# Sums of squares of two head norms taken as columns, with the squares as the stationary operand

## The reference, cut to what matters

```
y_m = mlstm_mixer(...)    # 4 heads of 64; h = rmsnorm(h, norm_g) over each head's 64 numbers
y_a = diff_attention(...) # 4 heads; rmsnorm of q and k over 64 numbers each, 4*2 heads each
y_h = hgrn2_mixer(...)    # 4 heads of 64; o = rmsnorm(o, norm_g) over each head's 64 numbers
x = x + concat(y_m, y_a, y_h) @ w_out
def rmsnorm(x, g): return x * rsqrt(mean(x*x, -1) + 1e-6) * g
```

## Time and profile before

| | us |
|---|---|
| median of 3 runs | 3740.42 (3738.63 to 3741.89) |
| profiled execution | 3740.01 |
| its span, first to last instruction | 3738.7 |
| mean granted TensorE clock | 0.941 of full |
| PE busy | 3434.8 (92%) |
| DVE, ACT, POOL busy | 1297.9, 1131.7, 1223.0 |

### The profile page before, as it was taken

How to read it: one execution, slowest core, us unless ns; L and a number is a source line. 1 busy time by engine, 2 the same in 40 slices (tenths; PEclk the granted TensorE clock), 3 DMA queues, 4 the chain that set the end, 5 groups by cost and what they waited for, 6 DMA issues and landing times.

```text
span 3738.7 us, 37076 instructions
## 1 busy us (share of the span) xinstructions
PE 3434.8 (92%) x15602; PEld 2733.0 (73%) x15602; DVE 1297.9 (35%) x2104; ACT 1131.7 (30%) x1552; POOL 1223.0 (33%) x305
## 2 busy tenths in 40 slices
PE   7887899998977899999998789998999989769999
PEld 5654588886744688888887678887888867548887
DVE  3336641214256431222124642123221253572122
ACT  2234332322234332322223232223222232423222
POOL 4210044343200244444443334443444432014443
PEclk9887799999977899999999899999999999879999
DMA  3210033332200133333322223323433323013332
GB/s 116 66 52 1 12 101 92 101 92 78 68 30 1 50 98 90 102 95 91 107 83 90 76 72 92 106 82 117 137 91 104 89 74 116 1 40 95 97 97 72
DMA packets 462184, 296.77 MB, mean 79 GB/s; under 512 B 14331, under 2 KB 454193, under 8 KB 462017
## 3 DMA queue, kind: packets, MB, share of 16 engines
q1 hardware_dynamic: 453664, 277.09, 25.5%
q10 hardware_dynamic: 8352, 17.30, 1.3%
HBM read 285.97 MB, written 8.39 MB: 79 GB/s over the span
## 4 chain that ended last, share of the span: by engine, by line
PE 82%; DVE 12%; ACT 3%; POOL 1%; issue 1%; DMA 0%; SPq 0%; ACTq 0%; DVEq 0%; POOLq 0%
PE bank L505 24%; PE bank L506 24%; PE bank L507 24%; PE bank L335 9%; DVE x L794 1%; DVE ta L792 1%; DVE ta L1177 1%; DVE xl L818 1%; POOL wlo L443 0%; DVE qkv L1972 0%; DVE sqacc L812 0%; DVE ta L1969 0%; DVE scr L1722 0%; DVE tiny L1465 0%; DVE u L689 0%
## 5 line engine op out<-in xcount | busy, mean ns | idle before, releaser
L443 POOL TENSOR_TENSOR wlo<-raw,whi 128x2048 fp32r<-128x2048 f32 (+4 forms) x283 | 1187.3, 4196 | 2348.3 <-ACT whi L428 2348.3
L505 PE MATMUL bank<-xh,whi 128*128 128x512 f32 x2432 | 971.4, 399 | 61.7 <-DVE xl L818 38.3
L506 PE MATMUL bank<-xl,whi 128*128 128x512 f32 x2432 | 958.5, 394 | 0.0
L507 PE MATMUL bank<-xh,wlo 128*128 128x512 f32 x2432 | 957.4, 394 | 0.0
L428 ACT ACTIVATE whi<-raw 128x2048 fp32r<-128x2048 f32 (+3 forms) x288 | 503.4, 1748 | 683.4 <-PE bank L507 648.5
L505 PEld LDWEIGHTS bank<-xh,whi 128*128 128x128 f32 x2432 | 463.7, 191 | 178.0 <-DVE xl L818 29.7
L507 PEld LDWEIGHTS bank<-xh,wlo 128*128 128x128 f32 x2432 | 463.0, 190 | 98.7
L506 PEld LDWEIGHTS bank<-xl,whi 128*128 128x128 f32 x2432 | 463.7, 191 | 93.0
L505 PE MATMUL bank<-ah,whi 128*128 128x512 f32 x1216 | 474.6, 390 | 5.2 <-POOL wlo L443 5.2
L506 PE MATMUL bank<-al,whi 128*128 128x512 f32 x1216 | 474.4, 390 | 0.0
L507 PE MATMUL bank<-ah,wlo 128*128 128x512 f32 x1216 | 474.4, 390 | 0.0
(11 more groups left out here) (334 smaller groups left out, 3004.3 us busy)
## 6 DMA issues: line engine op xcount, KB each, us to landing
raw<-in_ffn_w_gate SPq DMA_DIRECT2D x88, 512.0 KB, 4.0
raw<-in_ffn_w_up SPq DMA_DIRECT2D x88, 512.0 KB, 5.3
raw<-in_w_up SPq DMA_DIRECT2D x64, 512.0 KB, 4.8
raw<-in_w_down SPq DMA_DIRECT2D x64, 512.0 KB, 4.9
raw<-in_w_in SPq DMA_DIRECT2D x56, 512.0 KB, 4.7
raw<-in_ffn_w_down SPq DMA_DIRECT2D x64, 384.0 KB, 4.0
raw<-in_ffn_w_down SPq DMA_DIRECT2D x64, 320.0 KB, 3.5
raw<-in_w_out SPq DMA_DIRECT2D x16, 512.0 KB, 4.5
```

The lines of the kernel that those rows point to most:

```text
L443: g.e.tensor_tensor(self.wlo[slot][:, 0:n], self.raw[slot][:, 0:n], self.whi[slot][:, 0:n].bitcast(F32), ALU.subtract).then_inc(self.lo_ma ...
L505: pe.e.matmul(bank, hi[:, at:at + P], xh, start=k == ks[0], stop=False)
L506: pe.e.matmul(bank, hi[:, at:at + P], xl, start=False, stop=False)
L507: last = pe.e.matmul(bank, lo[:, at:at + P], xh, start=False, stop=k == ks[-1])
```

## The change

Where the buffers of squares hold all tiles (mLSTM, HGRN2), TensorE now makes the columns at once: for each block of 128 tokens and each of the two tiles, the squares (128 features by 128 tokens) are the stationary operand and four columns of `C_IND` stream through. That is 8 matmuls of 4 columns in place of 2 of 512 columns and 4 transposes, and the copy L1023 goes. Two turns are taken from each of these norms on each engine. The attention's norm keeps its way. The helper runs for mLSTM and for HGRN2 once in each layer, four times in all.

```diff
@@ act_rstd
         yield
-        yield
-        yield
+        if n < len(tiles):
+            yield
+            yield
         a.wait_ge(v_sig, v_sig[(*tag, "means")])
@@ pe_rstd
         for first in range(0, len(tiles), n):
             yield
             pe.wait_ge(a_sig, a_sig[(*tag, "squares", first)])
+            if n == len(tiles):
+
+                for b in range(NB):
+                    for j in range(n):
+                        last = self.mm(ps[:, b * w:b * w + w], squares[j][:, b * P:b * P + P], self.const[:, C_IND, 16 * j:16 * j + w],
+                                       b == 0 and j == 0, b == NB - 1 and j == n - 1)
+                last.then_inc(pe_sig.tick(*tag, "columns"), 1)
+                continue
...
-        yield
-        pe.wait_ge(v_sig, v_sig[(*tag, "sums")])
-        for b in range(NB):
-            last = pe.e.transpose(ps[:, b * w:b * w + w], rows[0:w, b * P:b * P + P], self.const[0:w, C_IDENT, 0:w])
-        last.then_inc(pe_sig.tick(*tag, "columns"), 1)
+        if n < len(tiles):
+            yield
+            pe.wait_ge(v_sig, v_sig[(*tag, "sums")])
+            for b in range(NB):
+                last = pe.e.transpose(ps[:, b * w:b * w + w], rows[0:w, b * P:b * P + P], self.const[0:w, C_IDENT, 0:w])
+            last.then_inc(pe_sig.tick(*tag, "columns"), 1)
@@ dve_rstd
-        v.wait_ge(pe_sig, pe_sig[(*tag, "sums", first)])
-        v.e.tensor_copy(rows[0:w, :], ps[0:w, :]).then_inc(v_sig.tick(*tag, "sums"), 1)
-        yield
-        yield
+        if n < len(tiles):
+            v.wait_ge(pe_sig, pe_sig[(*tag, "sums", first)])
+            v.e.tensor_copy(rows[0:w, :], ps[0:w, :]).then_inc(v_sig.tick(*tag, "sums"), 1)
+            yield
+            yield
         v.wait_ge(pe_sig, pe_sig[(*tag, "columns")])
```

## The result

| | before | after |
|---|---|---|
| median (12 runs each) | 3739.28 (3736.08 to 3747.87) | 3748.81 (3744.15 to 3752.58) |
| ratio, 95% interval | | 1.0024 [1.0016, 1.0032] |
| profiled execution, its span | 3740.01, 3738.7 | 3748.93, 3747.6 |
| mean granted clock | 0.941 | 0.936 |

The prediction was 3736.0, with a range up to 3744. The time lies outside it, and it moved the other way. It is the number of rival (c), 3748.

A forecast was written before the change was run, and what follows sets the result against it. PE holds 82% of the chain, but the norms are chains of hand-overs with no engine full. A layer: -1.2 - 3.6 + 2.55 = -2.25 us, two layers -4.5, so 3735.5 profiled, 3736 as median; range 3729 to 3744.

The forecast's parts named there:

- rival (c): Lag exposed for both head pairs (5.1 us), near products ahead of the heads' transposes: +8.0 us in all, 3748; chance 0.09.
- The sums themselves: Both norms: new sums cost 1.9 (mLSTM) and 3.4 us (HGRN2), like the old; PE saves only the transposes, 0.4 to 0.6.
- Term 1: mLSTM's norm: earlier sums and reciprocals let the last L1306 start 1.2 us sooner a layer; bounds 0 and 2.
- Term 2: Tail at HGRN2's norm: heads' products no longer wait for squares and sums; L1011 3.6 us sooner a layer, bounds 1.7 and 3.9.
- My test for term 2: Term 2 is wrong if third block's transposes to `out`, 26.1 us, shrinks by less than 2 us.
- Term 3: HGRN2 lags the heads by about one level: hidden beside heads 0 and 1, 2.55 us exposed beside 2 and 3; bounds 0, 5.1.
- The prediction's own sign of being wrong in this term: Maxima of heads 2 and 3 come no later against mLSTM's end than before, or over 4 us later.

The follow-up runs named there:

- e8: Kernel before with columns made at once in mLSTM's and HGRN2's norms, every turn kept, so no other stream's instruction changes place; 3747.34 us, 1.0012 of before.
- g3: Changed kernel with two idle turns ahead of the attention's norm (no lag) and two ahead of HGRN2's norm; 3736.65 us, 0.9984 of before.
- g2: Kernel before with columns for HGRN2's norm alone and two idle turns ahead of that norm, mLSTM's norm as before; 3736.07 us, 0.9984 of before.
- e4: Kernel before with two idle turns ahead of HGRN2 on every engine, so it lags the heads, no columns; 3751.38 us, 1.0022 of before.
- g1: Kernel before with two idle turns ahead of HGRN2's norm, old sums and transposes kept; 3738.77 us, 0.9989 of before.
- g4: g3 with its two idle turns behind the attention's norm instead of ahead, so HGRN2 lags in that norm alone; 3743.12 us, 1.0000 of before.

## Why the prediction was wrong, point by point

**The sums themselves: right, but for what follows them.** 16 records in 1.96 and 1.90 us, within the 1.9 to 3.4 given; mLSTM's in layer 1 took 2.80. HGRN2's I took at 3.4, it was 1.90 in both layers (the second below); in e8, at a clock of 0.50, it was 3.57, so the estimate of 1.7 us at either clock does not hold at the lower one. That the products behind the sums could run at another clock for it, as they do in e8, stood in no term.

**Term 1: right in mechanism and size, worthless in effect.** Counted from the squares, the sum had L1011 at 11.8 us, L1035 at 13.7 and the last L1306 at 22.5; the rows above give 11.66, 13.64 and 22.22, a gain of 1.43 us against 1.2. But in g3, where the two turns stand idle behind it, 0.3 to 0.6 us of it are left at the heads, and g2, without it, is no slower.

**Term 2: right at its head, partly lost at its end.** From the third block's transposes to the heads' products it is 1.18 us, as forecast (1.17); to L1011 it is 432.49 - 421.55 = 10.94 us, where it was 14.29: 3.35 sooner, forecast 3.6. From there to `out` the code is the same, but before it took 11.78 us in layer 0 and 9.10 in layer 1, after it 12.73 in both. Layer 1 before:

```profile
1236.42 1.06 PE L1011 MATMUL bank<-const,scr 128*4 128x128 f32 x4
1238.25 1.12 PE L335 MATMUL bank<-scr,sel 4*128 4x512 f32 x2 [0.77 <-DVE scr L1035]
1239.30 2.05 PE L335 MATMUL bank<-u 128*128 128x128 f32 x16
1241.28 1.12 PE L335 MATMUL bank<-scr,sel 4*128 4x512 f32 x2
1245.52 0.76 PE L505 MATMUL bank<-mh,whi 128*128 128x512 f32 x1 [3.12 <-DVE ml L1306]
```

And after:

```profile
1235.57 1.90 PE L335 MATMUL bank<-const,scr 128*128 128x4 f32 x16
...
1240.87 1.06 PE L1021 MATMUL bank<-const,scr 128*4 128x128 f32 x4
1242.70 2.07 PE L335 MATMUL bank<-scr,sel 4*128 4x512 f32 x2 [0.77 <-DVE scr L1046]
1244.70 3.78 PE L335 MATMUL bank<-u 128*128 128x128 f32 x16
1248.41 2.07 PE L335 MATMUL bank<-scr,sel 4*128 4x512 f32 x2
1253.60 0.76 PE L505 MATMUL bank<-mh,whi 128*128 128x512 f32 x1 [3.12 <-DVE ml L1317]
```

The same three groups took 0.95 + 1.73 + 0.95 = 3.63 us more, each near twice as long: a granted clock of 0.50 where it was 1.00. That is more than the 3.13 us that the tail had gained at its head in this layer. My test for term 2 (26.1 us shrinks by under 2) is passed in layer 0, where it shrinks to 23.67. In layer 1 it fails: 23.70 before (from 1221.82), 24.20 after (from 1229.40). Without the lag the gain of the place does arrive: 0.9984 and 0.9982.

**Term 3: the step that failed.** It had a lag of one level at 2.55 us a layer, all of it beside heads 2 and 3, bounded by 5.1. The runs put the lag at 3748.81/3739.28 against g3's 0.9984, so 0.41%, some 15 us or 7.7 a layer (the intervals leave 5 us either way on the 15); e4 against g1 gives 12 to 15. The prediction's own sign of being wrong in this term, maxima of heads 2 and 3 over 4 us late, is met in layer 0 (5.6 to 9.3) and not in layer 1. The lag has three places:

- The attention's norm, 3.1 us by order and up to 1.6 by the clock. The prediction did not charge it at all. I had moved the heads against HGRN2, but the attention's norm moves with them, and there the lag puts a level in front of the spreading. The diff of the instruction order showed it; I looked for the level only on DVE and among the heads.
- Heads 0 and 1: nothing (3.1 to 3.3 in the table, layer 0). Here the prediction was right, for the reason given: their third maxima are 5.8 us late, and the tables, which now come behind the third block, give 2.5 of it back.
- Heads 2 and 3. The level ahead of the maxima is there as forecast. DVE after, layer 0:

```profile
393.67 0.42 DVE L1720 TENSOR_TENSOR scr<-u,scr 128x256 f32<-128x256 f32 x1
394.00 0.42 DVE L1721 TENSOR_TENSOR scr<-u,scr 128x256 f32<-128x256 f32 x1
394.34 1.32 DVE L1733 COPY_PREDICATED scr<-level,bank 128x512 f32<-128x512 uint8 x2
395.56 0.87 DVE L1476 TENSOR_REDUCE tiny<-bank 128x1 f32<-128x128 f32 x4
...
402.66 1.33 DVE L1733 COPY_PREDICATED scr<-level,bank 128x512 f32<-128x512 uint8 x2 [2.23 <-PE bank L335]
403.89 0.67 DVE L1738 TENSOR_TENSOR scr<-scr,u 128x512 f32<-128x512 f32 x1
...
405.33 0.76 DVE L1476 TENSOR_REDUCE tiny<-bank 128x1 f32<-128x256 f32 x2 [0.17 <-PE bank L335]
...
409.37 0.48 DVE L1488 SCALAR_TENSOR_TENSOR u<-u,tiny 128x256 f32<-128x256 f32 x1
```

It costs 1.2 us at the first maxima and 0.95 more at the second (0.4 in layer 1). What came on top is what I had priced under rival (c) and given 0.09. The weights of the second block are ready at 409.85, and PE then has this ahead of their transposes:

```profile
410.02 2.88 PE L335 MATMUL bank<-scr,u 128*64 128x128 f32 x16 [0.69 <-ACT scr L1819]
412.83 0.80 PE L335 MATMUL bank<-u,scr 128*128 128x128 f32 x2
413.42 0.73 PE L1419 MATMUL bank<-const,u 128*128 128x128 f32 x4
```

Before, the same products had run beside the exponentials, and the transposes started as soon as the weights were there:

```profile
401.53 1.58 PE L335 MATMUL bank<-scr,u 128*64 128x128 f32 x16 [0.69 <-ACT scr L1808]
403.04 0.49 PE L335 MATMUL bank<-u,scr 128*128 128x128 f32 x2
...
404.48 0.48 DVE L1477 SCALAR_TENSOR_TENSOR u<-u,tiny 128x256 f32<-128x256 f32 x1
...
405.02 0.44 PE L1408 MATMUL bank<-const,u 128*128 128x128 f32 x2 [0.36 <-DVE u L1477]
```

That is 413.42 - 409.85 = 3.6 us of exposure, of which 2.8 show at the third maxima. Not all of it is order: 1.30 + 0.31 = 1.6 us are the clock, 0.50 here and 1.00 before. In layer 1 the exposure is 3.5 us, and only 0.3 of it shows, since there the stretch from the weights to the third maxima had run at 0.68 before and took 5.36 us, for 3.92 in layer 0. Against this rival I had argued that the products ran ahead of the scores before. That was read from heads 0 and 1 (322.28); beside heads 2 and 3 they ran behind the scores of the second block, where PE had nothing else to do.

**The sum.** Terms 1 and 2 without the lag measure -6 us (g3), for -9.6; the lag measures +15, for +5.1. -6 + 15 = +9, and the change measures +9.5. (The 15 is the difference of the change and g3, so this shows where the two parts lie and not that they add up; without any columns g1 measured -4 and e4, which is g1 with the lag, +11, each beside its own runs of before.) How much of the 15 is order and how much the clock that came with it stays open: of the places above only the norm's 3.1 us are cleared of the clock. Rival (c) had the right total and one of the right mechanisms (the near products), but 5.1 us for the pairs where 2 were, and not the norm. So it was right by half, and its total by luck.

**The range** went wrong with term 3: its upper bound of 5.1 a layer took the lag as one level's work on DVE, and not as what each queue does at every place where the two lines meet. It did not even take in its own bounds together: no gain from mLSTM, the lesser tail and 5.1 of lag give +3.4 a layer, 3746.8.

## What to carry to other kernels

Where queues are filled by stepping generators in turn, a shorter helper is two changes: the operation, and the shift of everything behind it. Price the shift by going through every engine's order at every later meeting point, the nearest first, and put idle steps back where the operation was to see the two apart. Here the operation gained nothing that could be measured, and at the old place of HGRN2's sums it cost some 2 us a layer by the clock behind it (e8); the shift cost 15 us. The two turns given back and the sums of HGRN2 placed behind the last scores make the version that beats both (3736.65 and 3735.88 us, 0.9984 and 0.9982 of before), and the old sums at that place give most of it.

## What the runs showed of the hardware

The same instructions in the same order take different times in the two layers of one execution, by the clock that each stretch is granted. In g4 the windows of the mixers are

```profile
246.98:442.30 195.32, 135.80 (x697) 83.45 (x697) 119.74 (x274) 86.84 (x172) 0.00 (x0) 0.72 0.01 4
1057.27:1247.99 190.72, 132.99 (x697) 83.36 (x697) 119.53 (x274) 86.77 (x172) 0.00 (x0) 0.74 0.01 4
```

4.6 us apart at 0.72 and 0.74. A single profile of a stretch with many short waits is good to some 5 us, as large as most terms of my sum; the medians and the comparison of both layers are what the conclusions above rest on. Keeping PE busier with matmuls of 64 rows and 64 columns did not raise the clock (0.68 to 0.70). And two ways to make the same sums, of nearly the same length (4 records of 512 columns in 3.35 us, 16 records of 4 columns in 3.57), were followed by different clocks: 1.00 and 0.96 before, 0.50 to 0.63 in all ten layers with the columns at that place.
